# A two-block transformer on one core: the last two tiles ahead of each norm by token halves, feed-forward groups of 14 and 8 chunks

## Chip, core and metric

The kernel runs on one core of one Trainium2 chip. The metric is the device time of one execution in microseconds (us). Lower is better. 0.2% of it is about 8 us.

## What is computed

Two token streams with 1024 features each: `lat` with 512 tokens, `ctx` with 256. The first block, on `lat` alone, has two layers. In each of them a SwiGLU feed-forward (2816 wide), a mixer and a second feed-forward are added to the stream, each with a modulated gate, and each sum goes through a layer norm and, for the next input, a modulation whose vectors come from `ada_w`:

```python
h = modulate(x, mod[:, 0, 0], mod[:, 0, 1])
y = swiglu_ffn(h, ffn1_w_in[l], ffn1_w_out[l])
x = layer_norm(ALPHA * x + 0.5 * mod[:, 0, 2] * y, ln_g[l, 0], ln_b[l, 0])
...
x = layer_norm(ALPHA * x + mod[:, 1, 2] * y, ln_g[l, 1], ln_b[l, 1])
...
def layer_norm(x, g, b):
    mu = jnp.mean(xf, axis=-1, keepdims=True)
    var = jnp.mean(jnp.square(xf - mu), axis=-1, keepdims=True)
    return ((xf - mu) * lax.rsqrt(var + LN_EPS) * g + b).astype(x.dtype)
```

The second block has grouped-query attention and an MLP (4096 wide) on both streams, then latent attention and an MLP on `lat`, again with a norm behind each. All in float32.

## The kernel before

**Numbers.** A float32 product is made of three passes on TensorE with rounded operands: weights low by input high, high by low, high by high (`passes`, lines 1934, 1935, 1936). For this ScalarE rounds each weight unit from `raw` to `w_hi` (line 1262) and VectorE subtracts, `w_lo = raw - w_hi` (`split_weights`, line 2750; 2048 columns). There are two slots of `w_hi`/`w_lo`, so a unit's split can begin only when TensorE has left the unit two before it. Inputs are held as `h_hi`/`h_lo` (`hc_` for `ctx`), the feed-forward's inner values as `hid_hi`/`hid_lo`.

**Tiles and units.** Features lie on partitions, tokens along the free dimension. A chunk is 128 input features, a tile 128 output features of all tokens; a linear's output of 1024 features is 8 tiles. A weight unit holds `tpu` tiles of `kc` chunks. The feed-forward's 22 chunks are worked in `FF_GROUPS`, 12 and then 10: first the gate and up products of a group, then its part of the output, `ffn_out`, with `tpu` 1, `kc` 12 or 10 and so 8 units. The other linears ahead of a norm (`mix_out`, `gqa_o`, `mlp_out`, `mla_o`) have 4 units of two tiles with 8 chunks each. Between the two groups of the last feed-forward, ctx is taken in (`ctx_in`): GpSimd scales x_ctx (line 1071), VectorE and ScalarE make `hc_`.

**A linear ahead of a norm** (`linear_then_norm` on ScalarE and VectorE, `then_norm` on TensorE). VectorE adds each finished tile to x (`tile`, line 3142). The sums of the norm are prepared from x shifted by the mean of tiles 0 to 3: GpSimd adds these (line 1027), TensorE's `first_mean` multiplies the sum by ones, ScalarE writes `m_lat` (line 1401), VectorE subtracts it (`shifted`, line 3015), ScalarE squares, GpSimd adds squares up (line 1042), VectorE adds up tiles 4 to 6 (`shifted_sums`, line 3030). Tiles 0 to 6 are worked with all tokens; tile 7 by halves of 256 tokens, called parts (`lat` has two, `ctx` one). A part's totals are matmuls with ones in plain float32 (`totals_begun`, lines 1950, 1955 and 1958, and `close`, lines 1966 and 1969).

**The norm** (`apply`), per part: take over tile 7 (`last_tile`, line 3042), `deviation` (lines 3053, 3055, 3058, ScalarE's root), `inverse` (line 3065), and then, per group of 1, 1, 2, 2, 2 tiles, `centred` (line 3076), `scaled` (line 3087), ScalarE's affine to `h_hi`, GpSimd's copy of the same (line 1056), and the split `h_lo` (line 3095), for which TensorE waits. Between them VectorE and ScalarE prepare the next linear's first unit (`ahead`), and its second, in two halves (`second_unit_half`, line 2770), where that linear has one stream and is worked by halves (`halved`). The order within each engine is written out by hand, the same in all ten norms.

**TensorE behind a norm** (`linear`, inner function with `wide`). With one stream (`wide` 2) it does part 0 with the whole first unit and half the second, then part 1; with two streams or one unit (`wide` 1) it does the first unit part by part: first the `ctx` part where it is older (`before_it`), then `lat` halves, then `ctx`.

## Time and profile before

| | us |
|---|---|
| median of three runs | 3994.9 (3991.51 to 4000.39) |
| span of the profiled execution | 3992.6 |
| TensorE busy | 3831.8 (96%) |
| VectorE busy | 2539.0 (64%) |
| ScalarE busy | 1385.7 (35%) |
| GpSimd busy | 561.8 (14%) |

The span goes from the first to the last recorded instruction of one execution, which is not one of the three timed; of its own total time only the span is listed. Busy time on TensorE includes passes that wait in the pipeline, so 96% isn't the engine at its peak. The chain of work that ended last is 81% TensorE and 13% VectorE. A row of the timeline is start, duration, engine, line, operation, what is written and read, count, and in brackets the idle time of the engine ahead of it with what ended it. PEclk is the clock granted to TensorE as a share of its full 2.4 GHz; 0.50 is its other level, 1.2.

### The profile page before, as it was taken

What the parts mean: (1) busy time and instruction counts of PE and PEld (TensorE: products, weight loads), DVE (VectorE), ACT (ScalarE), POOL (GpSimd) and SP (SyncE); (2) the same over time, 40 slices, a digit from 0 to 9 for tenths busy, and PEclk for the clock granted to TensorE, in tenths of its full rate; (3) what the DMA queues carried; (4) which work ended last, traced back from release to release, by engine and by line L of the source; (5) the groups of instructions that cost most, each with busy time, mean ns of one, the idle gap of its engine ahead of it and who ended that gap; (6) DMA issues with size and microseconds to landing.
All of it is one profiled execution on the core that took longest, in us unless ns stands there. A gap on an engine that the chain in (4) does not pass through costs nothing.

```text
span 3992.6 us, 51437 instructions
## 1 busy us (share of the span) xinstructions
PE 3831.8 (96%) x20234; PEld 3226.3 (81%) x20234; DVE 2539.0 (64%) x4095; ACT 1385.7 (35%) x1994; POOL 561.8 (14%) x559
## 2 busy tenths in 40 slices
PE   8999999999999999999998988989999999999998
PEld 6888877888888888788887678878888887888886
DVE  4666776754674677778445489686665367866335
ACT  2222334322232224432123179431221234853223
POOL 1000402300120012130004200150000141113001
PEclk8999999999999999999999999999999989999999
DMA  4554212344343432125322011213322112322221
...
DMA packets 71229, 415.97 MB, mean 104 GB/s; under 512 B 8928, under 2 KB 12128, under 8 KB 30048
## 3 DMA queue, kind: packets, MB, share of 16 engines
q1 hardware_dynamic: 69744, 406.63, 29.3%
...
## 4 chain that ended last, share of the span: by engine, by line
PE 81%; DVE 13%; ACT 2%; issue 2%; POOL 2%; DMA 0%; DVEq 0%; ACTq 0%; POOLq 0%
PE ps L1934 25%; PE ps L1936 24%; PE ps L1935 24%; DVE nmax L3716 2%; PE ps L1928 1%; DVE w_lo L2750 1%; PE ps L2644 1%; POOL sq_h_lat L1056 1%; DVE gp_lo L3733 1%; DVE rstd_lat L3065 1%; DVE x_lat L3076 1%; DVE x_lat L3087 1%; DVE mp_lo L3733 1%; DVE gprob L3728 1%; PE ps L2173 1%
## 5 line engine op out<-in xcount | busy, mean ns | idle before, releaser
L1934 PE MATMUL ps<-h_hi,w_lo 128*128 128x512 f32 (+2 forms) x2872 | 1096.6, 382 | 71.5 <-DVE h_lo L3095 49.6
L1936 PE MATMUL ps<-h_hi,w_hi 128*128 128x512 f32 (+2 forms) x2872 | 1073.0, 374 | 0.0
L1935 PE MATMUL ps<-h_lo,w_hi 128*128 128x512 f32 (+1 forms) x2800 | 1046.3, 374 | 0.0
L1262 ACT ACTIVATE w_hi<-raw 128x2048 fp32r<-128x2048 f32 (+3 forms) x262 | 457.8, 1748 | 1367.7 <-PE ps L1936 1329.7
L2750 DVE TENSOR_TENSOR w_lo<-raw,w_hi 128x2048 fp32r<-128x2048 f32 (+3 forms) x262 | 558.5, 2132 | 576.4 <-ACT w_hi L1262 576.1
L1934 PEld LDWEIGHTS ps<-h_hi,w_lo 128*128 128x128 f32 (+1 forms) x2872 | 548.9, 191 | 181.4 <-DVE h_lo L3095 46.0
L1936 PEld LDWEIGHTS ps<-h_hi,w_hi 128*128 128x128 f32 (+1 forms) x2872 | 548.3, 191 | 95.8
L1935 PEld LDWEIGHTS ps<-h_lo,w_hi 128*128 128x128 f32 x2800 | 535.5, 191 | 87.4 <-issue 0.5
L2836 DVE SCALAR_TENSOR_TENSOR ada_acc<-raw,c_act,ada_acc 128x256 f32<-128x256 f32 x1141 | 499.9, 482 | 16.8
L1934 PE MATMUL ps<-hid_hi,w_lo 128*128 128x512 f32 (+1 forms) x1272 | 498.9, 392 | 8.7 <-DVE w_lo L2750 6.8
L1936 PE MATMUL ps<-hid_hi,w_hi 128*128 128x512 f32 (+1 forms) x1272 | 490.2, 385 | 0.0
L1935 PE MATMUL ps<-hid_lo,w_hi 128*128 128x512 f32 (+1 forms) x1272 | 489.8, 385 | 0.0
L1934 PEld LDWEIGHTS ps<-hid_hi,w_lo 128*128 128x128 f32 x1272 | 240.1, 189 | 62.8 <-DVE w_lo L2750 8.9
L1936 PEld LDWEIGHTS ps<-hid_hi,w_hi 128*128 128x128 f32 x1272 | 239.7, 188 | 51.6
L1935 PEld LDWEIGHTS ps<-hid_lo,w_hi 128*128 128x128 f32 x1272 | 240.2, 189 | 50.4 <-issue 1.2
L1027 POOL TENSOR_TENSOR x_sum_lat<-x_lat 128x512 f32<-128x512 f32 x10 | 14.1, 1412 | 1867.2 <-DVE x_lat L3142 1319.4
L3142 DVE SCALAR_TENSOR_TENSOR x_lat<-ps,mod_lat,x_lat 128x512 f32<-128x512 f32 x70 | 52.4, 749 | 183.4 <-PE ps L1936 177.7
L1056 POOL TENSOR_SCALAR sq_h_lat<-x_lat,mod_lat 128x256 f32<-128x256 f32 x144 | 132.8, 931 | 173.5 <-DVE x_lat L3087 173.5
L3716 DVE TENSOR_REDUCE nmax<-ps 128x1 f32<-128x768 f32 x160 | 134.7, 842 | 8.2 <-PE ps L1936 5.7
L1304 ACT ACTIVATE hid_hi<-val_t 128x512 f32 (+1 forms) x88 | 55.6, 632 | 225.2 <-DVE val_t L2798 225.2
L1934 PE MATMUL ps<-hc_hi,w_lo 128*128 128x256 f32 x424 | 122.5, 289 | 8.2 <-DVE hc_lo L3095 8.2
L1440 ACT ACTIVATE h_hi<-x_lat,mod_lat 128x256 fp32r<-128x256 f32 x144 | 79.7, 594 | 128.8 <-DVE x_lat L3087 128.8
...
## 6 DMA issues: line engine op xcount, KB each, us to landing
...
```

The source lines that it names most:

```text
L1056: eng.tensor_scalar(h32[:, k, part.cs], x[:, k, part.cs], g[:, k:k + 1], b[:, k:k + 1], ALU.mult, ALU.add).then_inc(s_n32, 1)
L1262: eng.activation(w_hi[:, slot, 0:ln.width], raw[:, slot, 0:ln.width], ACT.Copy).then_inc(s_whi, 1)
L1304: eng.activation(hid_hi[:, at(i), :], val_t[:, pos % 2, 0:SEQ].unsqueeze(1), ACT.Copy)\
L1440: eng.activation(hi[:, k, part.cs], x[:, k, part.cs], ACT.Identity, bias=b[:, k:k + 1], scale=g[:, k:k + 1]).then_inc(s_nhi, 1)
L1934: eng.matmul(out, lo_w, hi_x, start=first, stop=False, skip_group_check=True)
L1935: eng.matmul(out, hi_w, lo_x, start=False, stop=False, skip_group_check=True)
L1936: return eng.matmul(out, hi_w, hi_x, start=False, stop=last, skip_group_check=True)
L2750: eng.tensor_tensor(w_lo[:, slot, 0:ln.width], raw[:, slot, 0:ln.width], w_hi[:, slot, 0:ln.width].bitcast(F32), ALU.subtract).then_inc(s_ ...
L2836: ins = eng.scalar_tensor_tensor(acc, weights[:, :, k, :], c_act[:, c:c + 1], acc, ALU.mult, ALU.add)
L3142: a = eng.scalar_tensor_tensor(x, ps[:, tile_bank(ln, m, st), 0:NT[st]], MODT[st][:, ln.gate[st], 2 * DC + m:2 * DC + m + 1], x, ALU.mult, ...
L3716: eng.reduce_max(nmax[:, k % 8:k % 8 + 1], flat(2 * (k % 2))[:, 0:nk], AX_X, negate=True).then_inc(t_mx, 1)
L3733: eng.tensor_tensor(a.p[1][:, k % NPT, :], ps[:, B_PT + k % 2, :], a.p[0][:, k % NPT, :].bitcast(F32), ALU.subtract).then_inc(t_pl, 1)
```

## The change

1. `FF_GROUPS` becomes (14, 8). `ffn_out` of the second group has 4 units of two tiles with 8 chunks (as `mlp_out` has) and four banks of sums instead of two; that of the first has 8 units of 14 chunks. Memory for it comes from `base`. `linear` now looks past `ctx_in` for the linear ahead of it.
2. Ahead of each norm tiles 6 and 7 are both worked by token halves: part 0 of both, then part 1 of both. A part's totals are six ones-matmuls in place of five: `sums` and `sums_of_squares`, the former with x_sum, tile 6 and tile 7 apart, the latter likewise with squares.
3. `first_mean` stands inside tile 4. VectorE's `shifted` of tiles 0 to 3, 6 and 7 stand ahead of tile 4's takeover and of the last unit's split; `shifted_sums` is done once.
4. In `apply` each part begins with `deviation`, two `centred` and `inverse`. The second half of the last tiles is taken over, with one stream, behind all of the first half's groups, else behind its second group; the second weight unit's halves stand beside it.
5. With `wide` 2 TensorE does the first unit's chunks 0 to 5 with part 0, `sums`, half of the second unit's chunks 0 to 5, `sums_of_squares`, and then the rest. With `wide` 1 `sums` stands behind chunk 5 and `sums_of_squares` behind chunk 7.

```diff
-FF_GROUPS = (12, 10)
+FF_GROUPS = (14, 8)
...
+def out_tiles(g):
+
+    return 2 if g + 1 == len(FF_GROUPS) else 1
...
+            per = out_tiles(g)
+            lin(f"ffn{which}_out_{l}_{g}", DC // per, per, nc, "resid", src="hid")
...
+    if ln.g0 == 0 and lo < 10 < hi:
+        cuts.add(10)
...
+        def part_bank(ln, q, part):
+
+            nxt = ln.norm.next
+            if len(ln.streams) == 1 and nxt and len(nxt.streams) > 1:
+                return q if part.c0 else 2 + q
+            return tile_bank(ln, DC - 2 + q, part.st)
...
-                    if i == ln.n - 1 and ln.tpu == 2 or i == ln.n - 2 and ln.tpu == 1:
+                    if i == ln.n - 1:
...
+            def sums(norm, j):
+
+                part, ns = norm.parts[j], len(norm.streams)
+                c, bank = part.cs, B_SUM[j]
+                eng.wait_ge(s_csum, w.csum + ns)
+                eng.matmul(ps[:, bank, 0:HALF], ones[:, :], x_sum[part.st][:, c], start=True, stop=False, skip_group_check=True)
+                eng.wait_ge(s_evac, part_evac(norm, j, 0))
+                eng.matmul(ps[:, bank, 0:HALF], ones[:, :], X[part.st][:, DC - 2, c], start=False, stop=False,
+                           skip_group_check=True)
+                eng.wait_ge(s_evac, part_evac(norm, j, 1))
+                eng.matmul(ps[:, bank, 0:HALF], ones[:, :], X[part.st][:, DC - 1, c], start=False, stop=True,
+                           skip_group_check=True).then_inc(s_total, 1)
...
+            def sums_of_squares(norm, j):
...
-                eng.matmul(ps[:, B_SQ, 0:HALF], ones[:, :], ssum[part.st][:, c], start=True, stop=False,
+                eng.matmul(ps[:, B_SQ, 0:HALF], ones[:, :], ssum[part.st][:, c], start=True, stop=False, skip_group_check=True)
+                eng.wait_ge(s_sq7, 2 * part.nidx + 1)
+                eng.matmul(ps[:, B_SQ, 0:HALF], ones[:, :], squares_of(norm, part.st)[:, DC - 2, c], start=False, stop=False,
                            skip_group_check=True)
-                eng.wait_ge(s_sq, w.sq + 4 * ns)
...
+                eng.wait_ge(s_sq7, 2 * part.nidx + 2)
+                eng.matmul(ps[:, B_SQ, 0:HALF], ones[:, :], squares_of(norm, part.st)[:, DC - 1, c], start=False, stop=True,
+                           skip_group_check=True).then_inc(s_total2, 1)
...
                     for n, p in enumerate(parts):
                         if p in norm.parts and len(ln.streams) > 1:
-                            eng.wait_ge(s_evac, last_evac(norm, len(norm.parts) - 1 if before_it else norm.parts.index(p)))
-                        if p in norm.parts and closing[:1] == [2]:
-                            totals_begun(norm, 2)
+                            eng.wait_ge(s_evac, part_evac(norm, max(1, norm.parts.index(p)), 1))
...
+                            if wide > 1 and k == DC - 2:
+                                sums(norm, n + 1)
+                                eng.wait_ge(s_wlo2, ln.halved)
+                                eng.wait_ge(s_evac, part_evac(norm, 1, 1))
+                                for i in range(k):
+                                    pair(1, p, i, (0,))
+                                sums_of_squares(norm, n + 1)
...
+                            if wide == 1 and p in norm.parts and closing:
+                                if k == DC - 3:
+                                    sums(norm, closing[0])
                                 if k == DC - 1:
-                                    pair(1, p, k - 1, (0,))
-                                pair(1, p, k, (0,))
...
+                                    sums_of_squares(norm, closing.pop(0))
...
+                                if m == 4 and k == (5 if len(ln.streams) == 1 else 6) and st == "lat":
+                                    first_mean(norm)
...
-                        if m == 4:
-                            first_mean(norm)
...
+                    eng.wait_ge(s_wlo, ln.g0 + ln.n)
                     for j, part in enumerate(norm.parts):
...
+                        for q in range(2):
+                            m = DC - 2 + q
+                            if j == 0:
+                                eng.wait_ge(s_evac, ln.e0 + m - ln.nbuf + 1)
+                            elif part_bank(ln, q, part) == part_bank(ln, q, norm.parts[j - 1]):
+                                eng.wait_ge(s_evac, part_evac(norm, j - 1, q))
+                            else:
+                                eng.wait_ge(s_evac, tile_evac(norm, DC - 3))
+                            for k in range(ln.kc):
+                                if j == 1 and q == 0 and k == 2:
+                                    sums(norm, 0)
+                                if j == 1 and q == 0 and k == 4:
+                                    sums_of_squares(norm, 0)
+                                mm = part_mm(ln.n - 1, q, part, k, part_bank(ln, q, part))
+                            mm.then_inc(s_tile if j + 1 == len(norm.parts) else s_last, 1)
                     if not norm.next:
-                        close(norm, len(norm.parts) - 1)
+                        sums(norm, 1)
+                        sums_of_squares(norm, 1)
...
-                        linear(ln, sched[j - 1][1] if sched[j - 1][0] == "lin" else None, norm, before_it)
+                        prev = next(i for i in sched[j - 1::-1] if i[0] != "ctx_in")
+                        linear(ln, prev[1] if prev[0] == "lin" else None, norm, before_it)
...
-            def shifted_sums(norm, k):
+            def shifted_sums(norm):
...
+                    eng.wait_ge(s_cent, w.cent + 3 * ns + i + 1)
+                    eng.tensor_tensor(x_sum[st][:, :], X[st][:, 4, :], X[st][:, 5, :], ALU.add).then_inc(s_csum, 1)
+
+            def last_tile(ln, j, q):
+
...
-                last_tile(ln, 0)
+                last_tile(ln, 0, 0)
                 if norm.next:
                     ahead(norm.next, 0, 1)
-                deviation(norm, 0)
-                centred(norm, 0, 0)
-                centred(norm, 0, 1)
-                inverse(norm, 0)
+                last_tile(ln, 0, 1)
+                halves = norm.next and norm.next.halved is not None
                 for j, part in enumerate(parts):
+                    more = j + 1 < len(parts)
+                    early = more and j == 0 and not halves
+                    deviation(norm, j)
+                    centred(norm, j, 0)
+                    centred(norm, j, 1)
+                    inverse(norm, j)
                     for g in range(len(GROUPS)):
                         scaled(norm, j, g)
                         if norm.next and g:
                             split_part(norm, part, g - 1)
-                        if g == 3 and j + 1 < len(parts):
-                            last_tile(ln, j + 1)
-                    if j + 1 < len(parts):
-                        deviation(norm, j + 1)
+                        if early and g == 1:
+                            last_tile(ln, j + 1, 0)
+                            last_tile(ln, j + 1, 1)
+                    if more and not early:
+                        last_tile(ln, j + 1, 0)
+                        last_tile(ln, j + 1, 1)
+                    if more and halves:
+                        second_unit_half(norm.next, 0)
                     if norm.next:
-                        split_part(norm, part, 4)
-                    halves = j == 0 and norm.next and norm.next.halved is not None
-                    if halves:
-                        second_unit_half(norm.next, 0)
+                        split_part(norm, part, len(GROUPS) - 1)
+                    if more and halves:
+                        second_unit_half(norm.next, 1)
                     elif j == 0 and norm.next:
                         ahead(norm.next, 1, 2)
-                    if j + 1 < len(parts):
-                        inverse(norm, j + 1)
-                    if halves:
-                        second_unit_half(norm.next, 1)
...
-                    elif m == 4:
-                        eng.wait_ge(s_evac, tile_evac(norm, 3))
-                        shifted(norm, (0, 1))
                     elif m == 5:
                         eng.wait_ge(s_evac, tile_evac(norm, 5))
-                        shifted(norm, (2, 3))
-                        shifted_sums(norm, 5)
-                    elif m == 6:
-                        shifted_sums(norm, 6)
+                        shifted(norm, (2,))
+                        shifted_sums(norm)
 
                 for i in range(2, ln.n):
                     for m in range((i - 2) * ln.tpu, (i - 1) * ln.tpu):
                         tile(m)
-                    split_weights(ln, i, 0, i)
-                for m in range((ln.n - 2) * ln.tpu, (ln.n - 1) * ln.tpu):
-                    tile(m)
-                for m in range((ln.n - 1) * ln.tpu, DC - 1):
-                    tile(m)
+                    if i + 1 < ln.n:
+                        split_weights(ln, i, 0, i)
+                eng.wait_ge(s_evac, tile_evac(norm, 3))
+                shifted(norm, (0, 1, 3))
+                tile(DC - 4)
+                split_weights(ln, ln.n - 1, 0, ln.n - 1)
+                tile(DC - 3)
```

VectorE ahead of the first norm, from the takeover of tile 4 (L3142; L3155 after) on. L3015/L3034 is `shifted`, L2750/L2769 a weight split, L3030/L3042 `shifted_sums`, L3042/L3054 `last_tile`. Before:

```order
L3142 SCALAR_TENSOR_TENSOR x_lat<-ps,mod_lat,x_lat 128x512
L3015 TENSOR_TENSOR x_lat<-x_lat,m_lat 128x1024 x2
L2750 TENSOR_TENSOR w_lo<-raw,w_hi 128x1280
L3142 SCALAR_TENSOR_TENSOR x_lat<-ps,mod_lat,x_lat 128x512
L3015 TENSOR_TENSOR x_lat<-x_lat,m_lat 128x1024 x2
L3030 TENSOR_TENSOR x_sum_lat<-x_lat 128x512
L2750 TENSOR_TENSOR w_lo<-raw,w_hi 128x1280
L3142 SCALAR_TENSOR_TENSOR x_lat<-ps,mod_lat,x_lat 128x512
L3030 TENSOR_TENSOR x_sum_lat<-x_sum_lat,x_lat 128x512
L3042 SCALAR_TENSOR_TENSOR x_lat<-ps,mod_lat,x_lat 128x256
L2750 TENSOR_TENSOR w_lo<-raw,w_hi 128x2048
```

After:

```order
L3155 SCALAR_TENSOR_TENSOR x_lat<-ps,mod_lat,x_lat 128x512
L3034 TENSOR_TENSOR x_lat<-x_lat,m_lat 128x1024 x3
L3155 SCALAR_TENSOR_TENSOR x_lat<-ps,mod_lat,x_lat 128x512
L2769 TENSOR_TENSOR w_lo<-raw,w_hi 128x2048
L3155 SCALAR_TENSOR_TENSOR x_lat<-ps,mod_lat,x_lat 128x512
L3034 TENSOR_TENSOR x_lat<-x_lat,m_lat 128x1024
L3042 TENSOR_TENSOR x_sum_lat<-x_lat 128x512
L3054 SCALAR_TENSOR_TENSOR x_lat<-ps,mod_lat,x_lat 128x256
L2769 TENSOR_TENSOR w_lo<-raw,w_hi 128x2048
L3054 SCALAR_TENSOR_TENSOR x_lat<-ps,mod_lat,x_lat 128x256
```

Four shifts in one piece with the last unit's split behind them, where the splits stood between; the next linear's first unit (2048 columns) now stands between tile 6's and tile 7's first half.

VectorE in the first norm, around the takeover of the second half (L3042; L3054 after). L3095/L3107 is `h_lo`, L3053 to L3058 and L3065 to L3070 `deviation`, L2770/L2789 the second unit's halves, L3065/L3077 `inverse`. Before:

```order
L3042 SCALAR_TENSOR_TENSOR x_lat<-ps,mod_lat,x_lat 128x256
L3076 TENSOR_TENSOR x_lat<-x_lat,m_lat 128x2x256
L3087 TENSOR_TENSOR x_lat<-x_lat,rstd_lat 128x2x256
L3095 TENSOR_TENSOR h_lo<-sq_h_lat,h_hi 128x2x256
L3053 TENSOR_SCALAR m_lat<-ps 128x256
L3055 TENSOR_TENSOR rstd_lat<-m_lat 128x256
L3058 SCALAR_TENSOR_TENSOR rstd_lat<-ps,rstd_lat 128x256
L3095 TENSOR_TENSOR h_lo<-sq_h_lat,h_hi 128x2x256
L2770 TENSOR_TENSOR w_lo<-raw,w_hi 128x1024
L3065 RECIPROCAL rstd_lat<-rstd_lat 128x256
L2770 TENSOR_TENSOR w_lo<-raw,w_hi 128x1024
```

After:

```order
L3099 TENSOR_TENSOR x_lat<-x_lat,rstd_lat 128x2x256
L3107 TENSOR_TENSOR h_lo<-sq_h_lat,h_hi 128x2x256
L3054 SCALAR_TENSOR_TENSOR x_lat<-ps,mod_lat,x_lat 128x256 x2
L2789 TENSOR_TENSOR w_lo<-raw,w_hi 128x1024
L3107 TENSOR_TENSOR h_lo<-sq_h_lat,h_hi 128x2x256
L2789 TENSOR_TENSOR w_lo<-raw,w_hi 128x1024
L3065 TENSOR_SCALAR m_lat<-ps 128x256
L3067 TENSOR_TENSOR rstd_lat<-m_lat 128x256
L3070 SCALAR_TENSOR_TENSOR rstd_lat<-ps,rstd_lat 128x256
L3088 TENSOR_TENSOR x_lat<-x_lat,m_lat 128x256 x2
```

The takeover has moved behind the last group, with a half of the split on either side of the last `h_lo`.

TensorE in the first norm, while it works the second half of the last tiles; first the totals of the first half. Before (L1950, L1955, L1958 `totals_begun`, L1966 and L1969 `close`):

```order
L1950 MATMUL ps<-x_sum_lat,ones 128x256
L1955 MATMUL ps<-ssum_lat,ones 128x256
L1958 MATMUL ps<-sq_h_lat,ones 128x256
L1934 MATMUL ps<-hid_hi,w_lo 128x256
L1935 MATMUL ps<-hid_lo,w_hi 128x256
L1936 MATMUL ps<-hid_hi,w_hi 128x256
L1934 MATMUL ps<-hid_hi,w_lo 128x256
L1935 MATMUL ps<-hid_lo,w_hi 128x256
L1936 MATMUL ps<-hid_hi,w_hi 128x256
L1966 MATMUL ps<-x_lat,ones 128x256
L1969 MATMUL ps<-sq_h_lat,ones 128x256
```

After (L1951 to L1956 `sums`, L1966 to L1971 `sums_of_squares`):

```order
L1951 MATMUL ps<-x_sum_lat,ones 128x256
L1953 MATMUL ps<-x_lat,ones 128x256
L1956 MATMUL ps<-x_lat,ones 128x256
L1935 MATMUL ps<-hid_hi,w_lo 128x256
L1936 MATMUL ps<-hid_lo,w_hi 128x256
L1937 MATMUL ps<-hid_hi,w_hi 128x256
L1935 MATMUL ps<-hid_hi,w_lo 128x256
L1936 MATMUL ps<-hid_lo,w_hi 128x256
L1937 MATMUL ps<-hid_hi,w_hi 128x256
L1966 MATMUL ps<-ssum_lat,ones 128x256
L1968 MATMUL ps<-sq_h_lat,ones 128x256
L1971 MATMUL ps<-sq_h_lat,ones 128x256
```

Tile 6's and tile 7's values and squares are now multiplied apart, with two chunks between the sums and the squares.

## Rows read from the trace of the kernel before

**Rows 1.** TensorE's waits: who, released by whom, total us, times, longest us
```profile
PE ps L1934 <- DVE h_lo L3095: 49.6, 42, 4.4
...
PE ps L1934 <- DVE w_lo L2750: 16.2, 7, 6.0
```

**Rows 2.** Windows, tile 6 to third unit behind a norm, in four norms
```profile
core 0: us, PE busy (x) PEld busy (x) DVE busy (x) ACT busy (x) POOL busy (x), PEclk, DMA share, GB/s
429.40:478.20 48.80, 43.34 (x303) 39.55 (x302) 40.08 (x54) 20.55 (x29) 27.32 (x30) 1.00 0.24 84
697.30:744.70 47.40, 42.23 (x285) 39.24 (x284) 36.46 (x51) 20.87 (x30) 25.80 (x30) 0.93 0.19 67
1082.20:1132.40 50.20, 45.23 (x303) 41.59 (x303) 38.67 (x52) 21.99 (x31) 27.06 (x30) 0.93 0.33 123
3590.30:3637.80 47.50, 42.03 (x285) 39.16 (x284) 37.24 (x52) 20.48 (x30) 25.89 (x29) 0.93 0.13 45
```

**Rows 3.** Timeline of TensorE around the norm at 440 (start, duration, idle before in brackets)
```profile
436.77 0.38 PE L1934 MATMUL ps<-hid_hi,w_lo 128*128 128x256 f32 x1 [0.20 <-DVE w_lo L2750]
...
440.31 0.28 PE L1936 MATMUL ps<-hid_hi,w_hi 128*128 128x256 f32 x1
440.42 0.59 PE L1950 MATMUL ps<-x_sum_lat,ones 128*128 128x256 f32 x2
440.85 0.59 PE L1955 MATMUL ps<-ssum_lat,ones 128*128 128x256 f32 x2
...
448.86 0.36 PE L1934 MATMUL ps<-h_hi,w_lo 128*128 128x256 f32 x1 [1.27 <-DVE h_lo L3095]
```

**Rows 4.** Timeline of VectorE, same norm
```profile
444.20 0.42 DVE L3058 SCALAR_TENSOR_TENSOR rstd_lat<-ps,rstd_lat 128x256 f32<-128x256 f32 x1
...
457.77 1.22 DVE L2770 TENSOR_TENSOR w_lo<-raw,w_hi 128x1024 fp32r<-128x1024 f32 x1
```

**Rows 5.** Timeline of VectorE ahead of the norm at 3599
```profile
3580.68 2.33 DVE L2750 TENSOR_TENSOR w_lo<-raw,w_hi 128x2048 fp32r<-128x2048 f32 x1 [1.20 <-ACT w_hi L1262]
...
3585.73 2.36 DVE L3015 TENSOR_TENSOR x_lat<-x_lat,m_lat 128x1024 f32<-128x1024 f32 x2 [0.81 <-ACT m_lat L1401]
...
3591.30 3.15 DVE L3015 TENSOR_TENSOR x_lat<-x_lat,m_lat 128x1024 f32<-128x1024 f32 x2
```

**Rows 6.** The line L3015 over the whole kernel
```profile
L3015 DVE TENSOR_TENSOR x_lat<-x_lat,m_lat x40: 1210/1222/2057, 423.7 to 3961.8; 128x1024 f32<-128x1024 f32 x40
```

**Rows 7.** Timeline in the second ffn2, where ctx is taken in
```profile
2098.04 6.57 POOL L1071 TENSOR_SCALAR x_ctx<-x_ctx 128x256 f32<-128x256 f32 x8
2104.70 0.75 DVE L3142 SCALAR_TENSOR_TENSOR x_lat<-ps,mod_lat,x_lat 128x512 f32<-128x512 f32 x1 [5.72 <-POOL x_ctx L1071]
2106.90 0.79 PE L1934 MATMUL ps<-hid_hi,w_lo 128*128 128x512 f32 x1 [5.96 <-DVE w_lo L2750]
```

**Rows 8.** Windows: before and after the stall at 2101; norms with two streams; last norm
```profile
2086.80:2100.95 14.15, 14.14 (x61) 11.06 (x59) 6.75 (x11) 7.61 (x12) 8.61 (x12) 1.00 0.14 46
2106.90:2111.00 4.10, 4.10 (x10) 3.23 (x11) 2.01 (x2) 0.00 (x0) 2.44 (x1) 0.50 0.76 195
2138.40:2173.90 35.50, 30.08 (x204) 27.42 (x203) 29.62 (x40) 14.64 (x20) 13.59 (x13) 0.98 0.31 104
2600.20:2635.40 35.20, 29.45 (x197) 26.56 (x195) 32.03 (x45) 14.73 (x21) 15.09 (x16) 1.00 0.26 88
2635.40:2649.80 14.40, 10.02 (x52) 8.90 (x53) 11.81 (x21) 5.47 (x11) 7.68 (x9) 0.76 0.02 7
3191.90:3225.10 33.20, 30.54 (x196) 27.80 (x195) 29.86 (x44) 11.76 (x19) 14.70 (x16) 0.95 0.06 16
3959.00:3988.20 29.20, 16.94 (x93) 13.88 (x91) 22.95 (x36) 10.80 (x20) 4.75 (x4) 0.83 0.14 46
```

**Rows 9.** Timeline of VectorE in the last norm
```profile
3977.34 0.48 DVE L3042 SCALAR_TENSOR_TENSOR x_lat<-ps,mod_lat,x_lat 128x256 f32<-128x256 f32 x1
```

188 lines of the change are left out of this document (71 added, 117 removed).

## The prediction, on record before the changed kernel ran

> **What bounds the kernel now.** I read the waits of TensorE first: its largest entries are h_lo (the low half of the next linear's input, right behind a norm) and w_lo (the low half of a weight unit), the latter with one wait of 6.0 us [rows 1]. Everything else is matmuls in a row, so the end is set by TensorE, and the change is priced by what it does to TensorE's own time line. Then I measured, with windows, how long each norm takes from the first pass of tile 6 (of 8) to the first pass of the third weight unit behind the norm [rows 2]; then the passes and the VectorE instructions inside one such stretch [rows 3, 4], what stands on VectorE just ahead of one [rows 5, 6], the one long w_lo wait [rows 7], and the stretches of the norms with two streams and of the last norm [rows 8]. Times below are counted from the first pass of tile 6 unless a start time is given. The profiled span is 3992.6 and the median of the runs 3994.9; the sum is a difference, I take what lies around the span as unchanged, and so add it to the median.
>
> **Prices.** A pass 512 wide costs 0.232 (61 of them in 14.15) [rows 8], one 256 wide 0.12, and a ones-matmul (an exact f32 one, two entries in the trace) 0.43 (440.42 to 440.85) [rows 3].
>
> **The group change, (12,10) to (14,8).** The number of chunks is the same, so passes only move: in four norms two chunks of tile 6 (6 passes of 0.232) and of tile 7 (12 of 0.12) leave the stretch and are done in the first group, 2.83 us out of each stretch and none off the total. What changes is a wait. At 2098.04 POOL begins eight instructions on x_ctx (6.57 us); VectorE waits for them until 2104.70, its first evacuation stands in front of the split of the third weight unit, and TensorE, which is two units of one tile each ahead, stands from 2100.95 to 2106.90, 5.96 us [rows 7]. Behind it the granted clock is 0.50 for 4.1 us, 10 passes where 0.232 each would be 2.3 [rows 8]: 1.8 to 2.1 more. In the change a unit of the second group holds two tiles of eight chunks (48 passes, 11.1 us), so two units last 22.3 us from the start, 2086.80, that is until 2109.1; VectorE is free at 2104.7, evacuates two tiles (1.4) and splits 2048 columns (2.33 [rows 5]), ready at 2108.4. The margin is 0.7. So the 8.0 us go. first_mean now stands inside tile 4 and needs x_sum, which POOL adds only once it is free: I take +0.5 (0 to 1.5). **Term: -7.5** (bounds -8.0 and 0).
>
> **Last two tiles by halves, the order in one norm.** Before, tile 6 is 512 wide and tile 7 alone is halved. After: first half of 6 and 7 (48 passes, 5.7), then of the second half k 0,1 (0.7), three ones-matmuls (1.29), k 2,3 (0.7), three more (1.29), the last of which starts at 9.3; the second half is through at 14.0. That pair runs 0.6 [rows 3], so VectorE's L3058 can start at 9.97; from L3058 to the first chunk is 4.66 (444.20 to 448.86 [rows 3, 4]): first chunk at 14.6, a TensorE wait of about 0.6 where now it is 1.27 [rows 3]. The sixth ones-matmul of each part (0.43) is in these sums.
> Behind the first chunk the stretch now lasts 29.3 (448.86 to 478.20). After, the second half's six ones-matmuls stand there, two of which stand there now: +1.7. The gaps between groups stay, since VectorE's pace sets them, and the second half's first chunk arrives as TensorE comes to it (VectorE 18.0, TensorE 18.1): +1.0 for small gaps (0, if VectorE keeps ahead; 2.4, two halves of the split at 1.2 [rows 4], if both come between). So 32.1 behind it, 46.8 in all.
> **What stands ahead** is s, the time TensorE waits for the w_lo of the last unit, because three shifted instructions now stand in front of it on VectorE. From the norm at 3599: m_lat would be there at 3583.0 (its first_mean is 9 passes, 2.05, earlier, and m_lat is read at 3585.73 less 0.7), three shifts end at 3587.1, tile 4 at 3587.8, the split (2.33) at 3590.1, or 3590.7 with one POOL block; TensorE wants it at 3590.3 [rows 5]. So s = 0.3 (0 to 1.1); the 0.20 at 436.77 goes in return [rows 3].
>
> **Six norms with one stream on both sides** (the stretches in rows 2; the one at 1474.50 reads 48.80 like the first, the one at 1740.80 47.50 like the fourth). Less 2.83 where the groups change: the two FFN norms with clock 1.00 are 46.0 now and 47.1 after, +1.15 each, +2.3; the other four are 47.4, 47.4 (1082: 50.2 - 2.83), 47.5, 47.5, and 47.1 after, -1.3 together. These four show a granted clock of 0.93, the other two 1.00 [rows 2]: for a few us it is at its lower level, which costs 1.4 (47.4 against 46.0). With a wait of 0.6 in front of the first chunk, where now it is 1.27 even in a norm at 1.00 [rows 3], I expect that in one or two of six: +2.1 (0 to +8.4 for all six). **Term: +3.1.**
>
> **Norms with two streams behind or around them.** Their second weight unit is not brought forward (the code's `wide` is 1), and the sums of the next part now stand behind its sixth chunk and those of the squares behind its eighth, where now all stand behind the fourth. At 2149 (tile 6 at 2138.40): 35.5 - 2.83 = 32.7 to the second half's first chunk now; after 14.0 + 5.8 (the ctx chunks) + 8.4 (eight chunks and six ones-matmuls) + 4.9 + s = 33.4: +0.7. At 2611: 35.2 now [rows 8]; after 14.0 + 5.7 (ctx part of the tiles) + 8.4 + 4.9 + 1.5, since the shifts on both streams come late for the sums (0.8 to 2.5) = 34.5: -0.7. At 3203 the same 34.5 against 33.2: +1.3. From the second half's first chunk to the first ctx chunk it is 14.4 in both now; after, the eight chunks come at VectorE's pace (9.1 to the seventh, as at 448.86 in the first norm, and 1.4), then the squares, then 4.9 again: 17.3 (17.0 to 17.7), +2.9 each. **Terms: +0.7, +2.2, +4.2.**
>
> **The last norm.** Nothing follows on TensorE; the last scaled instruction on VectorE starts at 29.2 now [rows 8]. Its second half is taken over at 3977.34, 18.35 after tile 6 [rows 9]; after, at about 17.9: L3058 at 9.97 + s, 2.8 to the first scaled, 4.9 for the five groups; the second add costs 0.4, the two centred that now lie in front of the inverse, beside ScalarE's root, save 0.9, and the ones-matmuls find x_sum and tile 6 ready (0.5). **Term: -1.5** (-2.5 to 0).
>
> **Sum:** -7.5 + 3.1 + 0.7 + 2.2 + 4.2 - 1.5 = +1.2, so 3994.9 + 1.2 = **3996**. What is taken in front at the norms is paid again behind: TensorE does the same passes plus one ones-matmul for each of 22 parts (9.5 us, of which most lies where it would have waited).
>
> **Rivals.** (A) *Everything that waits is covered.* s = 0 (-2.4 over eight norms), the clock stays up in all six (-2.1), the sums don't wait in the two-stream norms (-3.0): 3996.1 - 7.5 = 3988.6, and 3986 if the last norm gives its 2.5 too. For it: the w_lo wait now is 0.20 only, and the first chunk comes with less wait. Against it: the margins on VectorE are tenths.
> (B) *The last unit's split comes late each time*, slower. The three shifts run while POOL adds the squares, on operands that both read. At 3591.30 two of them take 3.15, where the pair at 3585.73 takes 2.36 [rows 5], and over the kernel one takes 1.22 in the median and 2.06 at most [rows 6]. One blocked instruction more makes s = 1.1, two 1.9; TensorE then waits with the whole norm behind it, 8 norms x 0.8 to 1.6 = 6.4 to 12.8, with a clock that falls after it: about 4006. It decides from s = 1.1 on.
> The Trainium skill, page "SBUF — State Buffer", section "SBUF: two separate sides", says that VectorE with two SBUF inputs and a GpSimd instruction that reads SBUF lock a shared port pair against each other, for the whole of an instruction; the 3.15 in rows 5 agrees in kind. By that rule every shift that meets an add waits for its end, and rival B is the rule's result, 4006; by the median of rows 6 most don't meet one, and the forecast holds.
> (C) *The stall at 2100 stays.* If x_ctx comes over 0.7 later than now, TensorE stands again, behind unit 1; the 7.5 shrink by the delay, and with the clock's fall to near nothing: 4003.
>
> **How the numbers follow.** Forecast 0.48, (A) 0.26, (B) 0.15, (C) 0.08, and 0.03 for the rest. The forecast's own range, with each bound at half strength, is 3991 to 4001. The range for 8 in 10 reaches into A (whose own low end is 3983, with a first chunk that comes sooner than 14.6) and B: 3983 to 4008. A measurement of this kernel tells 0.2% (8 us) from no change, so faster is under 3987, slower over 4003. Under 3987: 0.16 of A, 0.08 of the forecast's bounds and 0.02 of the rest, 0.26. Over 4003: B, 0.04 of C, 0.08 of the forecast's and 0.01 of the rest, 0.28. Between: 0.46.
>
> **What the profile of the changed kernel would show.** The w_lo wait of 6.0 gone, the x_ctx row still 6.6. In each norm the first chunk at 14.6 to 15 behind tile 6, wait 0.4 to 0.9 instead of 1.3 to 2, the third unit at 47.1. A new small wait for w_lo in front of tile 6: under 0.5 speaks for me, over 1.1 for B. From the second half's to the ctx part's first chunk 17.3 instead of 14.4. The last scaled row at 27.7. I am wrong if VectorE's second half is far from ready when TensorE comes to it (a wait over 1 at the second half's first chunk), or if the clock falls in all six.

## The result, and the profile after

The change made the kernel slower: 4009.8 us in the median (4006.6 to 4022.3) against 3994.9. The ratio is 1.0047 with a 95% interval of 1.0033 to 1.0061; all intervals below are such. Measured again it was 4010.0, ratio 1.0045 (1.0031 to 1.0059). The first interval is 13 to 24 us more, where the prediction had +1 and a range up to 4008.

The profiled execution (span 4017.0) is one of the longer ones: its run took 4018.7, and the second profile, of a run of 4009.7, has a span of 4007.9. The page's span and first line:

```profile
span 4017.0 us, 51240 instructions
...
PE 3855.9 (96%) x20494; PEld 3257.5 (81%) x20494; DVE 2524.6 (63%) x4077; ACT 1381.4 (34%) x1988; POOL 587.2 (15%) x559
```

TensorE's waits (columns as in [rows 1]). The long w_lo wait of 6.0 in [rows 1] is gone; those of 4.7 were there before as the next longest. An entry stands here that the waits of before don't have, hid_lo, 3.9 us in four places:

```profile
PE ps L1935 <- DVE h_lo L3107: 48.0, 39, 4.8
...
PE ps L1935 <- DVE hc_lo L3107: 13.2, 8, 4.8
...
PE ps L1935 <- DVE w_lo L2769: 9.5, 2, 4.7
...
PE ps L1935 <- DVE hid_lo L2823: 3.9, 4, 1.4
```

The six norms with one stream, from the first pass of tile 6 to the third unit, as [rows 2] (the two that are not in that group are there too):

```profile
438.85:486.95 48.10, 42.88 (x313) 40.77 (x313) 37.08 (x52) 19.26 (x29) 28.24 (x30) 0.96 0.20 66
706.16:755.36 49.20, 44.20 (x313) 41.88 (x313) 35.82 (x50) 20.64 (x31) 28.27 (x30) 0.93 0.29 108
1097.04:1145.27 48.23, 43.13 (x314) 40.77 (x314) 35.68 (x50) 20.63 (x31) 28.52 (x30) 0.96 0.30 110
1491.02:1541.42 50.40, 45.31 (x314) 43.26 (x313) 37.01 (x52) 19.27 (x29) 29.69 (x32) 0.90 0.18 64
1760.67:1811.07 50.40, 45.31 (x313) 43.27 (x313) 36.04 (x50) 20.62 (x31) 29.69 (x32) 0.90 0.34 126
3613.92:3664.47 50.55, 45.53 (x313) 43.45 (x313) 36.43 (x51) 20.32 (x32) 29.75 (x31) 0.90 0.19 63
```

Together 296.9. Before, the same six are 290.2, less 2.83 in the three that follow a feed-forward 281.7: +15.2, where the forecast had +3.1. The granted clock is under 1.00 in all six, and at 0.90 in the last three, where the lowest of these six was 0.93 before.

Norms with two streams, as [rows 8]: tile 6 to the second half's first chunk at 2149; the same and from there to the first ctx chunk at 2611 and at 3203; and the last norm up to the last scaled instruction:

```profile
2156.54:2189.93 33.39, 28.54 (x217) 27.25 (x217) 26.77 (x38) 14.20 (x20) 16.36 (x14) 0.99 0.28 95
2619.83:2654.73 34.90, 28.81 (x219) 27.32 (x217) 26.99 (x41) 14.72 (x21) 15.42 (x16) 0.98 0.39 148
2654.73:2673.08 18.35, 12.31 (x61) 11.09 (x61) 12.43 (x22) 5.59 (x11) 7.11 (x9) 0.69 0.00 0
3215.09:3249.91 34.82, 28.68 (x219) 27.19 (x217) 24.77 (x40) 11.64 (x19) 15.33 (x15) 0.96 0.07 26
3249.91:3267.71 17.80, 11.75 (x61) 10.54 (x61) 12.43 (x22) 5.59 (x11) 7.09 (x9) 0.79 0.00 0
3985.74:4012.58 26.84, 16.83 (x121) 15.80 (x120) 21.16 (x35) 10.86 (x21) 6.07 (x4) 0.86 0.15 50
```

Against 32.7 (35.5 less 2.83), 35.2, 14.4, 33.2 and 14.4 they are +0.7, -0.3, +3.9, +1.6 and +3.4, together +9.4 (forecast +7.1). The last norm is 26.8 instead of 29.2, -2.4 (forecast -1.5).

TensorE inside the first norm, the answer to [rows 3]; the first chunk comes 15.2 after tile 6 (forecast 14.6 to 15), after a wait of 0.50 instead of 1.27. The next two waits are as before (0.90 and 1.7). The second half has two (0.51 and 1.38), where it had one of 1.0:

```profile
454.04 0.35 PE L1935 MATMUL ps<-h_hi,w_lo 128*128 128x256 f32 x1 [0.50 <-DVE h_lo L3107]
...
455.88 0.39 PE L1935 MATMUL ps<-h_hi,w_lo 128*128 128x256 f32 x1 [0.90 <-DVE h_lo L3107]
...
458.59 0.58 PE L1935 MATMUL ps<-h_hi,w_lo 128*128 128x256 f32 x1 [1.73 <-DVE h_lo L3107]
...
474.58 0.39 PE L1935 MATMUL ps<-h_hi,w_lo 128*128 128x256 f32 x1 [0.51 <-DVE h_lo L3107]
...
477.29 0.39 PE L1935 MATMUL ps<-h_hi,w_lo 128*128 128x256 f32 x1 [1.38 <-DVE h_lo L3107]
```

### The profile page after: what moved, and what is told of

It is laid out like the page before. It is cut to its first block, busy times and chain, and to the rows that moved or that the text cites. A ratio compares the mean times of both kernels' runs of the same rounds, so it can differ in the third digit from the quotient of the medians.

```text
span 4017.0 us, 51240 instructions
## 1 busy us (share of the span) xinstructions
PE 3855.9 (96%) x20494; PEld 3257.5 (81%) x20494; DVE 2524.6 (63%) x4077; ACT 1381.4 (34%) x1988; POOL 587.2 (15%) x559
## 4 chain that ended last, share of the span: by engine, by line
PE 82%; DVE 12%; POOL 2%; ACT 2%; issue 2%; DMA 0%; DVEq 0%; ACTq 0%; POOLq 0%
PE ps L1935 25%; PE ps L1936 24%; PE ps L1937 24%; DVE nmax L3726 2%; PE ps L1929 1%; PE ps L2662 1%; POOL sq_h_lat L1063 1%; DVE w_lo L2769 1%; DVE gp_lo L3743 1%; DVE mp_lo L3743 1%; PE ps L2191 1%; DVE gprob L3738 1%; DVE x_lat L3088 1%; DVE rstd_lat L3077 1%; ACT w_hi L1269 1%
## 5 line engine op out<-in xcount | busy, mean ns | idle before, releaser
L1935 PE MATMUL ps<-h_hi,w_lo 128*128 128x512 f32 (+2 forms) x2896 | 1110.4, 383 | 68.5 <-DVE h_lo L3107 48.0
L1937 PE MATMUL ps<-h_hi,w_hi 128*128 128x512 f32 (+2 forms) x2896 | 1084.1, 374 | 0.0
L1936 PE MATMUL ps<-h_lo,w_hi 128*128 128x512 f32 (+2 forms) x2816 | 1057.1, 375 | 0.0
L2769 DVE TENSOR_TENSOR w_lo<-raw,w_hi 128x2048 fp32r<-128x2048 f32 (+3 forms) x246 | 557.1, 2265 | 611.0 <-ACT w_hi L1269 610.8
L1935 PEld LDWEIGHTS ps<-h_hi,w_lo 128*128 128x128 f32 (+1 forms) x2896 | 560.4, 194 | 174.7 <-DVE h_lo L3107 38.2
L1937 PEld LDWEIGHTS ps<-h_hi,w_hi 128*128 128x128 f32 (+1 forms) x2896 | 560.1, 193 | 94.9
L1936 PEld LDWEIGHTS ps<-h_lo,w_hi 128*128 128x128 f32 (+1 forms) x2816 | 545.7, 194 | 87.2 <-issue 1.0
L1310 ACT ACTIVATE hid_hi<-val_t 128x512 fp32r<-128x512 f32 (+1 forms) x88 | 55.6, 632 | 232.0 <-DVE val_t L2817 232.0
L1937 PE MATMUL ps<-hc_hi,w_hi 128*128 128x256 f32 x424 | 122.2, 288 | 0.0
L1936 PE MATMUL ps<-hc_lo,w_hi 128*128 128x256 f32 x424 | 122.0, 288 | 0.0
```

What stands on the lines that cost most here:

```text
L1310: eng.activation(hid_hi[:, at(i), :], val_t[:, pos % 2, 0:SEQ].unsqueeze(1), ACT.Copy)\
L1935: eng.matmul(out, lo_w, hi_x, start=first, stop=False, skip_group_check=True)
L1936: eng.matmul(out, hi_w, lo_x, start=False, stop=False, skip_group_check=True)
L1937: return eng.matmul(out, hi_w, hi_x, start=False, stop=last, skip_group_check=True)
L2769: eng.tensor_tensor(w_lo[:, slot, 0:ln.width], raw[:, slot, 0:ln.width], w_hi[:, slot, 0:ln.width].bitcast(F32), ALU.subtract).then_inc(s_ ...
```

## Experiments

Twelve runs were made, the ninth of them of the changed kernel itself. A difference of two ratios has an interval of 5 to 8 us here, so most steps of 4 or 5 us below can't be told by the times alone; the stretches in the profiles show them. Two theories stood against each other at first. **Clock**: TensorE's granted clock falls in the norms, more often in the new order, and the loss is what the half level costs. **Structure**: the added ones-matmuls and later sums are simply on TensorE's path. A third question was where the groups' gain of 7.5 had gone.

**1. The groups alone**, on the norms of before.

```diff
-FF_GROUPS = (12, 10)
+FF_GROUPS = (14, 8)
...
+                    if ln.nbuf == 4 and last_bank(ln, norm.parts[0]) == 1:
+                        eng.wait_ge(s_evac, tile_evac(norm, 5))
```

> The kernel before with the feed-forward groups (14,8), two-tile units for the second group and the look past ctx_in; the norms stay as they were. If the groups bring what I forecast and all of the loss is in the norms: the wait of 6.0 us at 2100 is gone, 8 us less than before, about 3987, and its norms show the same stretches as before less 2.83 in four of them. If the groups themselves cost something elsewhere (the part before the first norm was 4.6 us later in the changed kernel by 85 us into the program, and feed-forwards another 4): 3993 to 3997, and the same 3 to 4 us at the first feed-forward pass.

Ratio 0.9995 (0.9985 to 1.0005), median 3989.5: 2 us less, 6 at most by the interval, not 8. The stall at 2100 is gone (longest w_lo wait 4.7), and the same four hid_lo waits, 3.9, are there. Its first feed-forward pass was at 47.7, in the changed kernel's profile at 54.1, in its second profile at 47.5 and before at 50.8: the start is a matter of the run, not of the groups. Two norms of it (from tile 7 on, since tile 6 has no marks of its own here):

```profile
699.32:741.37 42.05, 36.73 (x262) 34.78 (x260) 32.01 (x47) 17.89 (x28) 22.62 (x28) 0.92 0.21 76
3585.27:3626.94 41.67, 36.64 (x262) 34.65 (x260) 32.71 (x48) 17.51 (x29) 22.73 (x27) 0.92 0.15 51
```

**2. Small matmuls in the waits of the changed kernel.** Ones by ones into a bank that nobody reads, issued in front of the wait, so that TensorE works while it would stand; the first line with fill is for the second half, the other for the first.

```diff
+                    def fill(bank, n):
+                        for _ in range(n):
+                            eng.matmul(ps[:, bank, 0:P], ones[:, :], ones[:, :], start=True, stop=True,
+                                       skip_group_check=True)
...
+                                    fill(4, {0: 0, 1: 2, 2: 6}.get(k, 0))
...
+                                    fill(6, {0: 2, 1: 4, 2: 8}.get(k, 0))
```

> The changed kernel with small matmuls of ones by ones (128 columns, results not used) in front of the first groups' waits in the six norms with one stream: 2, 4 and 8 in the first half, 2 and 6 in the second, fewer than fit into the waits of 0.8, 1.1, 1.9, 0.8 and 1.7. Theory clock (TensorE's granted clock falls behind these waits, and that costs 14 us in the six stretches): the granted clock of the six windows goes from 0.90 to 0.96 to 1.00, and 8 to 14 us go. Theory structure (the waits and the added ones-matmuls are the loss): no change, or up to 2 us more.

All six stretches are at 1.00 and 47.4 to 47.5; the first, the fourth and the sixth:

```profile
430.30:477.83 47.53, 46.51 (x357) 44.32 (x357) 37.05 (x52) 19.27 (x29) 28.25 (x30) 1.00 0.19 67
1477.83:1525.25 47.42, 46.54 (x357) 44.31 (x357) 36.97 (x52) 19.28 (x29) 28.50 (x30) 1.00 0.18 68
3591.91:3639.36 47.45, 46.56 (x357) 44.38 (x358) 36.33 (x51) 20.23 (x32) 28.53 (x29) 1.00 0.18 68
```

So the clock is what made 48.1 to 50.6 of 47.45: 12.2 us in the first profile. Ratio 1.0034 (1.0021 to 1.0046) against 1.0047: 5 us less in the times, with an interval of 8, so that the times by themselves fit both theories. (The profiled run, 3993.8, is by 10 us the shortest of its six.) By the stretches the theory clock is right on the mechanism, and it isn't the whole: with the clock up in the six norms, the changed kernel is still 13 to 14 us slower than before (8 to 18 by the interval).

**3. Earlier sums with two streams.**

```diff
-                                if k == DC - 3:
+                                if k == 3:
                                     sums(norm, closing[0])
-                                if k == DC - 1:
+                                if k == 5:
                                     sums_of_squares(norm, closing.pop(0))
```

> The changed kernel, with two streams the sums behind the fourth chunk and those of the squares behind the sixth (they stand behind the sixth and the eighth). In three norms five waits of 5.1 us follow the squares at present. If the place of the sums makes these waits, each loses about 1.5 to 2.9 us, together 7 to 12 less than the changed kernel. If VectorE's own pace makes them (it is still at the part before), nothing moves, or the waits move to the sums.

In the changed kernel TensorE stands 4.8 in front of the second half and again in front of ctx:

```profile
2654.73 0.55 PE L1935 MATMUL ps<-h_hi,w_lo 128*128 128x256 f32 x1 [4.77 <-DVE h_lo L3107]
...
2673.08 0.55 PE L1935 MATMUL ps<-hc_hi,w_lo 128*128 128x256 f32 x1 [4.76 <-DVE hc_lo L3107]
```

With the sums earlier the longest of these is 4.1 and 3.3. The two norms, from the ctx part of tile 5 to the third unit, of the changed kernel and then of this one:

```profile
2616.96:2685.57 68.61, 53.35 (x349) 49.74 (x348) 48.56 (x74) 24.56 (x41) 35.82 (x38) 0.85 0.21 77
3212.22:3278.20 65.98, 51.43 (x349) 47.72 (x348) 46.71 (x73) 21.61 (x38) 33.70 (x34) 0.90 0.05 17
```

```profile
2602.98:2670.26 67.28, 54.05 (x350) 50.60 (x348) 48.68 (x74) 24.56 (x41) 36.40 (x39) 0.85 0.21 79
3197.00:3261.89 64.89, 54.34 (x349) 50.94 (x348) 47.01 (x73) 21.61 (x38) 34.14 (x35) 0.84 0.05 17
```

1.3 and 1.1 less, and 1.0 at 2149 (45.5 to 44.5): 3.4 in all, a third to a half of the 7 to 12 expected. It can be less: at 2149 the changed kernel's second profile has 44.7 without this edit, with the same wait of 4.8. The place of the sums made part of these waits; VectorE's pace makes the rest. The ratio, 1.0035 (1.0024 to 1.0046), agrees with that and also with the single-stream norms of this run, which happened to stay at 0.96 to 1.00 (together 285.9).

**4. Groups and small matmuls on the norms of before.**

> Groups (14,8) on the old norms, with the same small matmuls of ones in front of the waits in the six norms with one stream (5, 4, 8 and 1 in the first half, 5 in the second). Theory clock: the windows that show 0.93 go to 1.00, 1.4 us each in four norms, so 4 to 6 us under the groups alone: about 3982. Theory structure: the same as the groups alone.

Ratio 0.9985 (0.9976 to 0.9995), 4 us under the groups alone with an interval of 5 to 6 (by the medians, 3988.5 and 3989.5, only 1). All six are at 1.00 and 40.7, where the two rows of the first experiment have 42.05 and 41.67 at 0.92:

```profile
707.13:747.79 40.66, 39.74 (x307) 37.98 (x306) 31.99 (x47) 17.80 (x28) 22.88 (x28) 1.00 0.22 78
3594.34:3635.01 40.67, 39.76 (x308) 38.00 (x306) 32.74 (x48) 17.41 (x29) 23.02 (x27) 1.00 0.16 53
```

Now both orders can be compared without the clock. Old: 40.66, and 5.5 for tile 6 ahead of it (697.30 to 702.80) are 46.2. New: 47.45. So the new order is 1.25 us longer per norm, 7.5 in six. The prediction had 46.0 against 47.1.

**5. Five ones-matmuls per part instead of six**, on the second experiment. It leaves tile 6's squares out of the variance.

```diff
-                eng.wait_ge(s_sq7, 2 * part.nidx + 1)
-                eng.matmul(ps[:, B_SQ, 0:HALF], ones[:, :], squares_of(norm, part.st)[:, DC - 2, c], start=False, stop=False,
-                           skip_group_check=True)
```

> As the changed kernel with the small matmuls in the waits, and without the ones-matmul on tile 6's squares, so that each of 22 parts has five as in the kernel before (the variance then leaves out tile 6). If the sixth ones-matmul is on TensorE's path in every part: 22 x 0.43 = 9.5 less than with it, about 3995. If most of it lies where TensorE would wait (as the prediction said): 2 to 4 less, about 4001, and the stretches of single-stream norms go from 47.4 to 47.0.

```profile
430.31:476.99 46.68, 45.64 (x354) 43.54 (x353) 37.05 (x52) 19.27 (x29) 28.30 (x30) 1.00 0.20 68
3587.61:3634.22 46.61, 45.72 (x352) 43.65 (x353) 36.36 (x51) 20.60 (x32) 28.54 (x29) 1.00 0.20 68
```

46.6 instead of 47.45: 0.85, twice 0.43, in each single-stream norm, so both parts' sixth matmul is on the path there. In the long norms with two streams, which have three parts, it is 0.4 and 0.7 instead of 1.3 (68.6 to 68.2, 65.9 to 65.2): there some of it is hidden. The ratio falls from 1.0034 to 0.9999 (0.9988 to 1.0010), 14 us with an interval of about 7. 22 x 0.43 = 9.5 lies in it, and so do the 7.9 by which all norms together are shorter in the two profiles; 2 to 4 us doesn't.

**6. Small matmuls alone**, groups and norms of before.

> The kernel before (groups 12,10, old norms) with the small matmuls of ones in the waits of the six norms with one stream. Theory clock: the stretches that show 0.92 lose 1.4 each, four or five of six, so 5 to 7 less than before, ratio 0.9985. The groups (14,8) are then worth only the difference to the fourth run above: if about 2 to 3 us, the groups' gain of 7.5 is eaten by something else (a wait for hid_lo of 3.9 in four places, that stands only in kernels with these groups). If 7 to 8, it is not.

Ratio 0.9988 (0.9976 to 1.0000), median 3988.5, the same as the fourth. The stretches are at 1.00. The long stall stays (7 waits, longest 6.1):

```profile
PE ps L1934 <- DVE w_lo L2758: 16.3, 7, 6.1
```

So with the clock equal the times show no gain of the groups (1 us, with an interval of 6, in which a gain of some 4 could hide): the stall is gone, and the hid_lo waits come.

**7 and 8. All waits of the norms filled, and then the hidden value first.** The seventh adds small matmuls in the norms with two streams and the last one. The eighth also lets ScalarE and VectorE finish the last gate and up tile before they turn to the output's second unit (the same edit stands in the code of both):

```diff
-                    first = ln.events > ln.nbuf or (ln.events > 1 and i == ln.n - 1)
+                    first = ln.events > ln.nbuf or ((ln.events > 1 or ln.evac == "gateup") and i == ln.n - 1)
```

> Groups (14,8) on the old norms with the small matmuls also in the waits of the norms with two streams (18, 14 or 3 ahead of the second half, 10 ahead of ctx, 4 to 7 ahead of later groups) and in the last norm (16). Theory clock: the windows that show 0.84 to 0.88 over 40 to 57 us lose 1.4 to 4 us each, 6 to 10 us less than the fourth run, about 3980. Theory structure: no difference.

> As the last one, and in the feed-forwards ScalarE and VectorE do the last gate and up tile ahead of rounding and splitting the output's second unit (2048 columns wide now, 1280 before). If that split makes the four waits for hid_lo (3.9 us together), they go: 3 to 4 us less, and nothing in their place, since the second unit is wanted 11 us after the first. If the wait is for ScalarE's work alone, they stay.

The seventh: 0.9975 (0.9964 to 0.9986), 4 us under the fourth and 8 under the groups alone, the latter with an interval of 6, so that the small matmuls' gain is clear in the times too. The norm at 2611 was 56.5 at 0.88 in the first experiment; here both of that kind:

```profile
2599.65:2656.16 56.51, 42.84 (x271) 39.09 (x270) 46.52 (x71) 21.00 (x37) 30.73 (x35) 0.88 0.15 57
```

```profile
2598.76:2653.87 55.11, 49.53 (x369) 45.69 (x368) 46.47 (x71) 21.02 (x37) 31.06 (x35) 1.00 0.16 58
3190.66:3241.07 50.41, 46.83 (x347) 43.16 (x346) 44.58 (x70) 18.18 (x34) 29.00 (x30) 1.00 0.03 11
```

1.4 and (51.9 to 50.4) 1.5 less, a good deal under what was expected for them (1.4 to 4 each, 6 to 10 in all). The eighth: 3979.1, ratio 0.9959 (0.9945 to 0.9972), another 6 us less with an interval of 7. hid_lo, in the seventh still

```profile
PE ps L1942 <- DVE hid_lo L2832: 3.9, 4, 1.4
```

is not among its waits. In three of the four places nothing stands instead. In the fourth, the feed-forward in which ctx is taken in, 1.43 of hid_lo is replaced by 0.35 for a split and 1.04 for x_sum, which GpSimd adds up only once it is through with x_ctx (0.11 in the seventh), so of the 3.9 only some 2.5 are gained:

```profile
2117.39 0.50 PE L1942 MATMUL ps<-hid_hi,w_lo 128*128 128x512 f32 x1 [0.35 <-DVE w_lo L2778]
...
2124.27 1.13 PE L1950 MATMUL ps<-x_sum_lat,ones 128*128 128x512 f32 x2 [1.04 <-POOL x_sum_lat L1035]
```

This is what happens at the first of these places, on VectorE in the kernel before, and then on VectorE and TensorE in the changed one: the split stands ahead of the last value and its low half, for which TensorE now waits in the middle of the first output tile:

```profile
386.91 1.49 DVE L2750 TENSOR_TENSOR w_lo<-raw,w_hi 128x1280 fp32r<-128x1280 f32 x1 [3.96 <-ACT w_hi L1262]
```

```profile
403.95 2.29 DVE L2769 TENSOR_TENSOR w_lo<-raw,w_hi 128x2048 fp32r<-128x2048 f32 x1 [3.16 <-ACT w_hi L1269]
406.16 0.69 DVE L2817 TENSOR_TENSOR val_t<-ps,gate_t 128x512 f32<-128x512 f32 x1
407.54 0.69 DVE L2823 TENSOR_TENSOR hid_lo<-val_t,hid_hi 128x512 fp32r<-128x512 f32 x1 [0.70 <-ACT hid_hi L1310]
...
408.29 0.50 PE L1935 MATMUL ps<-hid_hi,w_lo 128*128 128x512 f32 x1 [0.99 <-DVE hid_lo L2823]
```

VectorE's split itself waits for ScalarE to round the same unit, and that is wider too (1.92 instead of 1.27). From the start of the rounding to the end of hid_lo it is 6.2 instead of 4.8, that is 1.4 later, and TensorE comes to the value 6 passes (1.4) sooner. Before, it came 1.7 after hid_lo was ready. 1.7 less twice 1.4 is the wait of 1.0, but for a tenth; by this working either of the two alone would have made no wait here.

**9. The changed kernel once more.**

> The changed kernel once more, for a narrower interval beside the runs of before of the same hour, and for a second profile. The first profile (4017.0) was of a run 9 us above the median: its first h pass is at 54.1, where other kernels with the same start show 47.6 to 54.0, and its six single-stream stretches hold 9 us of time at the lower clock. If that is chance, the second profile has stretches of 47.4 to 49 and the ratio is 1.0033 to 1.0045. If the clock's fall belongs to the new order, they are again at 48 to 50.5 and the ratio 1.0045 to 1.006.

Ratio 1.0045. Its six norms are together 296.9, as in the first profile, though not in the same places; three of them:

```profile
1092.39:1140.20 47.81, 42.71 (x313) 40.59 (x313) 35.55 (x50) 20.63 (x31) 28.49 (x30) 0.96 0.30 111
1485.93:1533.37 47.44, 41.72 (x313) 39.40 (x313) 36.97 (x52) 19.28 (x29) 28.52 (x30) 1.00 0.20 68
3604.90:3655.37 50.47, 45.44 (x313) 43.38 (x313) 36.44 (x51) 20.30 (x32) 29.75 (x31) 0.90 0.19 63
```

The tenth kernel's six are together 293.7, the third's 285.9; these two have the same code there as the changed kernel. The norm at 1485 stands at 1.00 with the very waits (1.74 and 1.38 the longest) behind which the others fell. Of the old order three profiles (before, first and eleventh) can be set against their 1.00 level in the same way: 5.3, 6.4 and 6.3 lost in six norms, 6.0 in the mean, against 12.2, 12.2, 9.0 and 1.2 of the new, 8.6 in the mean. So the new order loses 3 to 6 us more to it than the old in three profiles of four, and less in the fourth: how often the clock falls is also a matter of the run, and seven profiles give its mean price, 3 us, only roughly.

**10. Hidden value first in the changed kernel; 11. the same on the groups alone.** Both edits as in the eighth.

> The changed kernel with the last gate and up tile of a feed-forward ahead of the output's second unit on ScalarE and VectorE. The four waits for hid_lo (3.9 us) go: 3 to 6 us less than the changed kernel (the eighth run was 5.7 under the seventh). If in the changed kernel something else stands behind them, less than 2.

> Groups (14,8) on the old norms with hid first and no small matmuls. If the groups' 7.5 were eaten by the hid_lo waits, it is now 6 to 8 under before (0.998 to 0.9985), and the last run but four (0.9959) is this plus 8 us of clock. If not, 0.9995 as with the groups alone.

The tenth: 1.0036 (1.0023 to 1.0049) against 1.0045, median 4010.6 against 4010.0. The hid_lo waits are gone from the profile, but the times don't tell the two apart: inconclusive by itself. The eleventh: 0.9984 (0.9975 to 0.9993), median 3987.5, in the expected band, and 4 us under the groups alone with an interval of 5. No one of the three pairs (eighth and seventh, tenth and ninth, eleventh and first) is clear by itself; their weighted mean is 4.8 us less, with an interval of 3.7. So the hidden value first does save time, and the 2.5 of the waits lie in it.

**12. The new order at its best**: hidden value first, earlier sums, and small matmuls in the waits of all norms but the last.

> The changed kernel with all three: hid first, the earlier sums, and small matmuls in the waits of norms with one and with two streams. The new norm order at its best against the old at its best (0.9959). With 14 us of added time in the norms at full clock, less 3.4 by the earlier sums: 0.9959 + 0.0027 = 0.9985, about 3988. If the sums' places and the clock together made the order slower, it comes to 0.9965 or less.

0.9985 (0.9976 to 0.9994), just as expected, and 8 us by the medians, 10 by the ratios above the eighth kernel, which is the old order with the same help (and small matmuls in the last norm). The norms that have small matmuls are at 1.00; three of them:

```profile
2599.65:2665.10 65.45, 56.10 (x421) 52.48 (x420) 48.47 (x74) 24.57 (x41) 35.80 (x38) 1.00 0.21 81
3191.84:3254.50 62.66, 55.76 (x422) 52.31 (x420) 46.64 (x73) 21.62 (x38) 33.67 (x34) 1.00 0.06 18
3589.96:3637.41 47.45, 46.56 (x356) 44.40 (x357) 36.34 (x51) 20.22 (x32) 28.51 (x29) 1.00 0.20 68
```

Against the old order (55.1 and 50.4 of the seventh, plus 5.5 for tile 6; here less 2.9 for the ctx part of tile 5) the two long ones are 62.6 against 60.6 and 59.8 against 56.0: +2.0 and +3.8. With +7.5 in the six, -2.0 in the last and -1.2 at 2149 (43.9 against 39.6 + 5.5) that makes 10.1, which is the difference of the two kernels. So with the clock up in both the new order still costs some 10 us: the part of the theory structure is shown too.

The fastest kernel is the eighth: groups (14,8), old norms, small matmuls in the waits, hidden value first, 16 us under before.

## Why the prediction was wrong

- **The group change, term -7.5.** The stall and the half clock behind it went as worked out (from tile 6 at 1740.80 to tile 6 at 2138.40 it was 397.6, and from 1760.67 to 2156.54 it is 395.9, though 2.8 of passes and 2.9 of the longer norm came in: 7.4 less). The step that failed is the one not taken: of the moved split I followed only the third unit's, and not the wider rounding and split (1.92 and 2.29 instead of 1.27 and 1.49) of the second, which ScalarE and VectorE do ahead of the last hidden value, nor that TensorE comes to that value after 21 passes instead of 27. That is +3.9 in four places. Experiment 1 shows that the groups bring these waits, 8, 10 and 11 that the order of the work ahead of the last value makes them; width and fewer passes count alike there (1.4 each, worked out above; no run separates them). The term should have been about -3.6. The wait for x_sum that I priced at +0.5 is 0.2 here and comes out, with 1.0, only when the hid_lo wait ahead of it is gone.
- **One norm's order.** The order itself was well sized: 47.1 forecast, 47.45 measured at full clock; first chunk 14.6 to 15, measured 15.2. For s I had 0.3; TensorE's passes show no idle time in front of tile 6, but in all eight norms the weight load of its first pass waits 0.33 to 0.49 for w_lo, so the split lands just as it is wanted. But the sentence that the sixth ones-matmuls lie mostly where TensorE would have waited is wrong: experiment 5 gives their full price, 0.85, in each of the six. The wait in front of the first chunk that they were to fill is bounded by VectorE's chain behind the last of them, so each moves its end too.
- **The clock, +2.1 of the +3.1.** Here the largest part was lost. I tied the fall to the wait in front of the first chunk, and expected it in one or two of six since that wait shrinks. It shrank (0.50) and the clock fell in all six, in three twice. Each fall begins within 1 us of the end of one of the two longest waits: six times that of 1.73 in the first half, three times that of 1.37 in the second. The waits inside the first half's groups (0.90 and 1.73) stayed, and the second half, which had one wait of 1.0, has two (0.51 and 1.38). Measured, instead of 2.1, 12.2, 12.2 and 9.0 in three profiles, 1.2 in a fourth. Experiment 2 shows that it is the clock, and that it stays up when the waits are filled; why it falls behind the same waits in one norm and not in another is open.
- **Two streams, +7.1.** Measured +9.4; from the second half to ctx 18.3 and 17.8 for 17.3, at a clock of 0.69 and 0.79. The mechanism was right, a size was off.
- **The last norm**, -1.5: -2.4, within its bounds.
- **Rivals.** B, the late last split, did not come: the shifts ahead of it (L3034) now take 1.22 in the median and 1.43 at most, and it is never late by more than the tenths above. The trace of the changed kernel thus doesn't bear out the price that the lock rule of the Trainium skill, page "SBUF — State Buffer", section "SBUF: two separate sides", would have had there; what became longer is the next linear's first split, 3.07 at 443.05 where 2.28 is usual, beside GpSimd's sums of squares, and that is covered. C, the stall that stays, did not come either. A's 3986 takes the last norm's gain twice (1.5 of the 2.5 are in the forecast already; 3987.6 would be right), which changes no chance to speak of. Of my two signs of being wrong, the clock's fall in all six came; the wait over 1 at the second half's first chunk did not in these norms (0.40 to 0.51). What came is a mechanism I had priced as a small term, and one I hadn't seen.

The sum, by what was measured: groups -8 and +3.9, the six norms +7.5 at full clock and +3 (by the means above) to +6 (by the changed kernel's own two profiles) by the clock above the old order's own losses, two streams +9.4, last norm -2.4: +13 to +16, where the times give +15 by the medians and +18 by the second ratio. In the first profile (+24.4) the clock is 7 and the start 3.3 more. Some 4 us, between the norms, are left. They are of the size by which such stretches differ from run to run of one program: from the third unit behind the norm at 2149 to ctx in the next norm it is 414.9 in the changed kernel's first profile and 410.9 in its second.
